# State-space units of a hybrid decoder step: outputs kept feature-major, their norm taken from column sums

## The reference, cut to what matters

```python
def step(s, inp):
    xb, dtb, dab, bb, cb = inp
    cum = jnp.cumsum(dab, axis=1)
    seg = cum[:, :, None] - cum[:, None, :]
    lmask = jnp.exp(jnp.where(causal, seg, -jnp.inf))
    cbw = jnp.einsum('bign,bjgn->bijg', cb, bb)
    wgt = cbw[..., None] * lmask * dtb[:, None]
    y = jnp.einsum('bijgr,bjgrp->bigrp', wgt, xb)
    y = y + jnp.einsum('bign,bgrpn->bigrp', cb, s) * jnp.exp(cum)[..., None]
    wlast = jnp.exp(cum[:, -1:] - cum) * dtb
    s = s * jnp.exp(cum[:, -1])[..., None, None] + jnp.einsum('bjgr,bjgrp,bjgn->bgrpn', wlast, xb, bb)
    return s, y
...
ys = ys + w['ssd_d'][l][:, None] * xs
gated = ys * jax.nn.silu(s_z)
y_c = _rmsnorm(gated, ssd_norm_g)      # over the 256 features of a group
```

## Time and profile before

| | before |
|---|---|
| median of 3 runs | 2722.2 us |
| profiled execution, its own time | 2716.7 us |
| its span, first to last instruction | 2714.6 us |
| mean granted TensorE clock | 0.996 of full |
| PE busy | 2672.4 us (98%) |
| weight loads busy | 2625.4 us |
| DVE busy | 1976.1 us (73%) |
| ACT busy | 894.2 us (33%) |
| POOL busy | 1254.0 us (46%) |

### The profile page before, as it was taken

One profiled execution on the slowest core, in us unless ns is written; L12 is line 12 of the kernel. 1 busy time (PEld: TensorE's weight loads), 2 busy tenths in 40 slices (PEclk: granted clock), 3 DMA queues, 4 the chain that ended last, 5 costly groups with the idle time before them and its releaser, 6 DMA issues.

```text
span 2714.6 us, 51113 instructions
## 1 busy us (share of the span) xinstructions
PE 2672.4 (98%) x18801; PEld 2625.4 (97%) x18801; DVE 1976.1 (73%) x2490; ACT 894.2 (33%) x1428; POOL 1254.0 (46%) x732
## 2 busy tenths in 40 slices
PE   9999999999999999999999999999999999999997
PEld 9999999989999999999999999999999999999997
DVE  7658887478866676667946598875787766677778
ACT  4443241134322232223424432312343322232333
POOL 2334233222665666666433333232226666666663
PEclk9999999999999999999999999999999999999999
DMA  4324333321211111111223344244111111111112
GB/s 165 129 77 158 137 114 127 118 65 32 64 54 47 47 47 47 54 54 47 71 87 104 113 141 143 84 141 134 42 47 48 47 47 60 49 47 47 47 62 92
DMA packets 74103, 219.60 MB, mean 81 GB/s; under 512 B 18480, under 2 KB 20144, under 8 KB 72896
## 3 DMA queue, kind: packets, MB, share of 16 engines
q1 hardware_dynamic: 69584, 202.27, 23.0%
q10 hardware_dynamic: 4368, 15.33, 1.9%
HBM read 176.35 MB, written 41.73 MB: 80 GB/s over the span
## 4 chain that ended last, share of the span: by engine, by line
PE 66%; issue 14%; POOL 8%; DVE 8%; DMA 2%; ACT 1%; PEld 1%; POOLq 0%; DVEq 0%; SPq 0%; ACTq 0%
PE ps L909 20%; PE ps L911 19%; PE ps L910 19%; POOL sb_w_lo L812 6%; DVE sb_pt L1950 2%; DMA sb_w_raw<-w 1%; DVE sb_x L1940 1%; PE ps L1043 1%; POOL sb_w_raw L855 1%; POOL sb_wsum L844 1%; PE ps L1158 1%; PE ps L1078 1%; PE ps L1079 1%; POOL sb_w_raw L851 1%; PE ps L1080 1%
## 5 line engine op out<-in xcount | busy, mean ns | idle before, releaser
L812 POOL TENSOR_TENSOR sb_w_lo<-sb_w_raw,sb_w_hi 128x512 fp32r<-128x512 f32 (+1 forms) x348 | 633.6, 1826 | 428.3 <-ACT sb_w_hi L1738 420.6
L909 PE MATMUL ps<-sb_p_hi,sb_w_hi 128*128 128x258 f32 (+1 forms) x2528 | 728.9, 288 | 7.2 <-POOL sb_w_lo L812 6.6
L911 PE MATMUL ps<-sb_p_hi,sb_w_lo 128*128 128x258 f32 (+1 forms) x2528 | 726.4, 287 | 0.0
L910 PE MATMUL ps<-sb_p_lo,sb_w_hi 128*128 128x258 f32 (+1 forms) x2528 | 725.8, 287 | 0.0
L809 POOL TENSOR_TENSOR sb_w_hi<-sb_w_raw,sb_ones 128x1024 fp32r<-128x1024 f32 (+1 forms) x92 | 180.4, 1961 | 846.7 <-PEq L906 733.8
L909 PE MATMUL ps<-sb_h_hi,sb_w_hi 128*128 128x344 f32 x1632 | 533.7, 327 | 4.1 <-DVE sb_h_lo L1902 1.6
L910 PE MATMUL ps<-sb_h_lo,sb_w_hi 128*128 128x344 f32 x1632 | 522.5, 320 | 0.0
L911 PE MATMUL ps<-sb_h_hi,sb_w_lo 128*128 128x344 f32 x1632 | 521.1, 319 | 0.0
L909 PEld LDWEIGHTS ps<-sb_p_hi,sb_w_hi 128*128 128x128 f32 x2528 | 478.0, 189 | 8.9 <-POOL sb_w_lo L812 7.6
L910 PEld LDWEIGHTS ps<-sb_p_lo,sb_w_hi 128*128 128x128 f32 x2528 | 479.4, 190 | 0.0
L911 PEld LDWEIGHTS ps<-sb_p_hi,sb_w_lo 128*128 128x128 f32 x2528 | 478.2, 189 | 0.0
(11 more groups left out here) (334 smaller groups left out, 3678.5 us busy)
## 6 DMA issues: line engine op xcount, KB each, us to landing
sb_w_raw<-w SPq DMA_DIRECT2D x178, 512.0 KB, 3.9
proj<-sb_ev SPq DMA_DIRECT2D x56, 516.0 KB, 3.0
sb_rawx<-w SPq DMA_DIRECT2D x44, 512.0 KB, 3.5
sb_pt<-proj SPq DMA_DIRECT2D x20, 516.0 KB, 5.2
sb_raw<-proj SPq DMA_DIRECT2D x16, 516.0 KB, 4.8
sb_raw<-proj ACTq DMA_DIRECT2D x16, 516.0 KB, 4.3
sb_ch<-cumT SPq DMA_DIRECT2D x32, 256.0 KB, 4.1
sb_raw<-ssd_state SPq DMA_DIRECT2D x4, 1024.0 KB, 6.2
```

Of the source, the lines that this page charges most:

```text
L812: return nc.gpsimd.tensor_tensor(o, a, h.bitcast(F32), ALU.subtract)
L909: mm(o, wh, ah, start=first, stop=False)
L910: mm(o, wh, al, start=False, stop=False)
L911: return mm(o, wl, ah, start=False, stop=last)
```

## The change

The outputs of a state-space unit stay feature-major. In `b_ssd` the values are stationary (128 x 64 for one head) and the segment weights are streamed (128 columns); of two heads one writes PSUM partitions 0 to 63 and the other 64 to 127. The state is stationary in two halves of 128 features, with C streamed. The two gate transposes are gone, and the wait for the gates moves from PE to DVE. ACT makes one more exponential for each chunk, `E(c)`, the decay laid out by features, in two activations of 64 partitions, ahead of the four Relu. DVE no longer makes `skip`, and adds D times the values with two fused operations. ACT's squares are written over the gates. The tail of u = 2 and 3 is new (`tail_s`): a column sum of squares by 9 small matmuls, root and reciprocal, 9 transposes that spread the result over the partitions, one scaling from PSUM, then the split. The retention units keep their tail.

```diff
         def b_ssd(u, c):
             s = cols(c)
             pe.wait_ge(*sg.after("awork", (u, c)))
-            if c == 0:
-                pe.wait_ge(*sg.after("gate_act", u))
-            else:
+            if c > 0:
                 pe.wait_ge(*sg.after("bwork", (u, c - 1)))
             for h in range(4):
-                mm(ps[:, 6, 64 * h:64 * h + 64], W(c)[:, 128 * h:128 * h + 128], xdt(c)[:, 64 * h:64 * h + 64],
+                j, q = h // 2, slice(64 * (h % 2), 64 * (h % 2) + 64)
+                mm(ps[q, 6, 128 * j:128 * j + 128], xdt(c)[:, 64 * h:64 * h + 64], W(c)[:, 128 * h:128 * h + 128],
                    start=True, stop=True)
-            mm(ps[:, 6, 256:512], pt[:, 1, s], St, start=True, stop=True)
             for j in range(2):
-                nc.tensor.transpose(ps[:, 7, 256 + 128 * j:384 + 128 * j], pt[:, Z0[u] + j, s], ident)
+                mm(ps[:, 6, 256 + 128 * j:384 + 128 * j], St[:, 128 * j:128 * j + 128], pt[:, 1, s], start=True, stop=True)
             mm(ps[:, 7, 0:256], btok(c), xwl(c), start=True, stop=True).then_inc(*sg.on("b_done", (u, c)))
...
+        def tail_s(u):
+
+            pe.wait_ge(*sg.after("sq_ready", u))
+            for c in range(NCH + 1):
+                n = min(CHUNK, T - c * CHUNK)
+                ins = mm(ps[0:n, 7, c:c + 1], pt[:, Z0[u], c * CHUNK:c * CHUNK + n], ones[:, 0:1], start=True, stop=True)
+            ins.then_inc(*sg.on("tok_sum", ("ssd", u)))
+            weights_done()
+            run(PLAN[u]["t"])
+            pe.wait_ge(*sg.after("tok_rstd", ("ssd", u)))
+            for c in range(NCH + 1):
+                n = min(CHUNK, T - c * CHUNK)
+                ins = nc.tensor.transpose(rstd_wide[:, c * CHUNK:c * CHUNK + n], rr[0:n, c:c + 1].to_broadcast([n, P]),
+                                          ident[0:n, 0:n])
+            ins.then_inc(*sg.on("tok_spread", ("ssd", u)))
+            weights_done()
...
         def seg_exp(u, c):
 
             act.wait_ge(*sg.after(f"seg_loaded{c % 3}", (u, c)))
+            if c >= 3:
+                act.wait_ge(*sg.after("bwork", (u, c - 3)))
+            for q in range(2):
+                rows = slice(64 * q, 64 * q + 64)
+                ins = af(halves(E(c))[rows], W(c).rearrange("p (j q n) -> p j q n", j=2, q=2)[rows, :, q, :], ACT.Exp)
+            ins.then_inc(*line.step())
+            act.wait_ge(*line.last())
             for h in range(4):
...
         def square_s(u, c):
-            act.wait_ge(*sg.after("bwork", (u, c)))
-            if c > 0:
-                act.wait_ge(*line.last())
-            af(junk.rearrange("p (j n) -> p j n", j=2), xt(u)[:, :, cols(c)], ACT.Square,
-               accum_out=ss[:, c:c + 1]).then_inc(*line.step())
+            if c < NCH:
+                act.wait_ge(*sg.after("bwork", (u, c)))
+                rows = cols(c)
+            else:
+                act.wait_ge(*sg.after("ys_ready", u))
+                rows = d
+            af(pt[:, Z0[u]:Z0[u] + 2, rows], xt(u)[:, :, rows], ACT.Square).then_inc(*sg.on("sq_done", (u, c)))
...
         def b_work_s(u, c):
             dve.wait_ge(*sg.after("b_done", (u, c)))
-            t = xwl(c)
-            v.tensor_tensor(heads(t, 4), heads(ps[:, 6, 256:512], 4),
-                            tk_of(1, u, c).unsqueeze(2).to_broadcast([P, 4, 64]), ALU.mult)
-            v.tensor_tensor(skip(c), skip(c), ps[:, 6, 0:256], ALU.add)
+            t, o = halves(xwl(c)), xt(u)[:, :, cols(c)]
+            v.tensor_tensor(t, halves(ps[:, 6, 256:512]), halves(E(c)), ALU.mult)
+            for j in range(2):
+                stt(o[:, j, :], o[:, j, :], A("ssd_d", 2 * u - 4 + j), ps[:, 6, 128 * j:128 * j + 128], ALU.mult, ALU.add)
...
+            if c == 0:
+                dve.wait_ge(*sg.after("gate_act", u))
             dve.wait_ge(*line.last())
-            v.tensor_tensor(xt(u)[:, :, cols(c)], heads(t, 2), heads(ps[:, 7, 256:512], 2),
-                            ALU.mult).then_inc(*sg.on("bwork", (u, c)))
+            v.tensor_tensor(o, o, pt[:, Z0[u]:Z0[u] + 2, cols(c)], ALU.mult).then_inc(*sg.on("bwork", (u, c)))
...
+        def tail_s(u):
+            sum_squares(u, d, NCH).then_inc(*sg.on("sq_ready", u))
+            dve.wait_ge(*sg.after("tok_sum", ("ssd", u)))
+            v.tensor_scalar(rr[:, 0:NCH], ps[:, 7, 0:NCH], 1.0 / 256, EPS, ALU.mult, ALU.add)
...
+            v.reciprocal(rr[:, 0:NCH + 1], rr[:, 0:NCH + 1]).then_inc(*sg.on("tok_rstd", ("ssd", u)))
+            run(PLAN[u]["t"])
+            dve.wait_ge(*sg.after("tok_spread", ("ssd", u)))
+            for j in range(2):
+                o = xt(u)[:, j, :]
+                stt(o, o, A("ssd_g", 2 * u - 4 + j), rstd_wide, ALU.mult, ALU.mult).then_inc(*sg.on("scaled", (u, j)))
+            if u == 2:
+                conv_s(3, 0)
+            elif u == 3:
+                rope(4, 0)
+            for j in range(2):
+                dve.wait_ge(*sg.after("y_hi", (u, j)))
+                ins = v.tensor_tensor(y_lo[:, j, :], xt(u)[:, j, :], y_hi[:, j, :].bitcast(F32), ALU.subtract)
+            ins.then_inc(*sg.on("y_split", u))
```

More of the change, by code:

```diff
@@ L327, in build, with E, halves @@
     St, junk = ch[:, 3072:3328], ch[:, 3328:3584]
-    def skip(c):
-        return ch[:, 2816:3072] if c % 2 == 0 else skip2[:]
+    def E(c):
+        return (ch[:, 2816:3072], ch[:, 3328:3584], skip2[:])[c % 3]
+    def halves(ap):
+        return ap.rearrange("p (j n) -> p j n", j=2)
+    rstd_wide = ps[:, 4:7, :].rearrange("p a n -> p (a n)")[:, 0:T]
     def kd(c):
@@ L582, in prep_early @@
                 if u > 3:
-                    sp.wait_ge(*sg.after("ys_turned", u - 1))
+                    sp.wait_ge(*(sg.after("tok_sum", ("ssd", 3)) if u == 4 else sg.after("ys_turned", u - 1)))
                     step()
@@ L597, in prep @@
                 if u < 4:
-                    sp.wait_ge(*(sg.after("y_split", 1) if u == 2 else sg.after("ys_turned", 2)))
+                    sp.wait_ge(*(sg.after("y_split", 1) if u == 2 else sg.after("tok_sum", ("ssd", 2))))
                     step()
@@ L1517, in square_r @@
             ins.then_inc(*sg.on("sq_done", (u, c)))
[L1519 to L1529, removed]
+        def tail_s(u):
+            square_s(u, NCH)
             act.wait_ge(*sg.after("rr_ms", u))
-            n = NCH + 1 if u < 4 else 2 * NCH + 2
-            af(rr[:, 0:n], rr[:, 0:n], ACT.Sqrt).then_inc(*sg.on("rr_root", u))
+            af(rr[:, 0:NCH + 1], rr[:, 0:NCH + 1], ACT.Sqrt).then_inc(*sg.on("rr_root", u))
             if u == 2:
@@ L1536, in tail @@
             y_free(u)
+            for j in range(2):
+                act.wait_ge(*sg.after("scaled", (u, j)))
+                af(y_hi[:, j, :], xt(u)[:, j, :], ACT.Identity).then_inc(*sg.on("y_hi", (u, j)))
+        def tail(u):
+            act.wait_ge(*sg.after("sy_ready", u))
+            act.wait_ge(*sg.after("sq_done", (u, NCH - 1)))
+            for h in range(2):
+                ins = af(junk[0:8, 128 * h:128 * h + 128], ps[0:8, 6, 128 * h:128 * h + 128], ACT.Square,
+                         accum_out=ss[0:8, 16 + h:17 + h])
+            ins.then_inc(*sg.on("ss_done", u))
+            act.wait_ge(*sg.after("rr_ms", u))
+            n = 2 * NCH + 2
+            af(rr[:, 0:n], rr[:, 0:n], ACT.Sqrt).then_inc(*sg.on("rr_root", u))
+            y_free(u)
             yh, _ = Y(u)
-            g = A("ssd_g", 2 * u - 4, 2) if u < 4 else A("ret_g", 2 * (u - 4), 2)
+            g = A("ret_g", 2 * (u - 4), 2)
             r = RING["tail", u]
@@ L2085, in b_work_r, with sum_squares @@
                             ALU.mult).then_inc(*sg.on("o_gated", (u, c)))
+        def sum_squares(u, rows, c):
+            dve.wait_ge(*sg.after("sq_done", (u, c)))
+            return v.tensor_tensor(pt[:, Z0[u], rows], pt[:, Z0[u], rows], pt[:, Z0[u] + 1, rows], ALU.add)
         def decode_s(u):
@@ L2428, in _ @@
                     decode_r(u)
-                tail(u)
+                if u < 4:
+                    tail_s(u)
+                else:
+                    tail(u)
             def gp(m):
```

83 lines of the change are left out of this document (38 added, 45 removed).

## The result

The changed kernel takes **2731.3 us** (median of 8 runs, 2721.9 to 2735.4), the kernel before 2722.0 (8 runs, 2717.7 to 2727.1). The ratio is 1.0027, with a 95% interval of 1.0016 to 1.0038: slower by 7.3 us, at least 4.4 and at most 10.3. The forecast was 2726.6 with a range of 2715 to 2736: the time is inside. The likeliest outcome by its chances, a change of at most 0.2%, is just missed: it is 0.27%, with an interval that reaches to both sides of that line.

The account below looks back on a forecast made before the run. PE, busy for 98% of the span, was taken as the bound, with DVE next in the chunks. Chunks -10.2, first chunk +1.7, tails +6.5 and clock +6.4 made +4.4: 2722.2 + 4.4 = 2726.6 us, range 2715 to 2736.

Parts of the forecast that it names:

- Chunks, PE: PE in the 32 state-space chunks: head products cheaper, gate transposes gone, 0.32 us saved a chunk, -10.2 us.
- DVE follows; I charge nothing: State-space chunks: DVE, already full, loses its slack but follows PE's 0.32 gain; charged nothing, up to 2 us for the range.
- DVE becomes the bound of the chunks: Rival: DVE bounds the chunks, or the next units start late; +2 to +6 on the forecast, 2729 to 2733; chance 0.08.
- DVE: forecast -0.26 a chunk: DVE in the chunks: `skip` goes, its add becomes two fused operations of some 0.20 us each; net -0.26 us a chunk.
- First chunk: First chunk of u = 2: two activations and a wait lengthen PE's wait by 0.87 us in each layer, +1.7.
- Tails: Four tails of u = 2 and 3: wait +0.94, sums +1.9, turn back replaced by spread -1.2, +6.5 in all.
- Clock: After the four tails: idleness and one-column passes in a row lower the clock at nearly every one, 1.6 us each, +6.4.
- the second rival: Behind the tails: the clock falls twice at each; +10.8, 2733 us; chance 0.15.
- The first rival: In the tails: the clock stays up; -2.0, 2720.2 us; chance 0.15.
- at most +1 each: Behind the tails: DVE's two scalings delay the next unit's work by up to 2 us; charged nothing, at most +1 each.
- DVE's 1032-column work in the tail: Tails: DVE's sum of 1024 columns costs nothing, at most 0.3; its two scalings, some 1.15 us each, also charged nothing.
- 0.07: Rival in the chunks' head products: the two heads do not run side by side; sum +19.1, 2741 us; chance 0.07.

Follow-up runs that it names:

- experiment 2: Changed kernel with all four heads' products written by the same half of the array's columns, even heads' results left out: 2742.3 us, one run.
- experiment 3: Changed kernel with two head products of 128 stationary columns in place of four of 64, array left whole: 2728.0 us, one run.
- experiment 4: Changed kernel without the two extra exponentials, state product and DVE's share of it in each state-space unit's first chunk: 2723.0 us, ratio 0.9996 to the kernel before.
- experiment 1: Changed kernel with the four head products in the order 0, 2, 1, 3: 2728.8 us, ratio 1.0023 to the kernel before.
- experiment 5: Changed kernel with 12 unread filler matmuls of 344 columns ahead of PE's wait for the squares in each state-space tail: 2725.2 us, ratio 1.0009 to the kernel before.
- experiment 6: Changed kernel with one product of nine columns in place of the nine column sums, the wait kept: 2716.9 us, ratio 0.9979 to the kernel before.
- experiment 7: Changed kernel with one of the tail's two in pieces run before the column sums, on PE and DVE: 2713.9 us, ratio 0.9975 to the kernel before.
- Experiment 8: Kernel of experiment 7 with ones stationary and squares streamed, no spreading transposes, root and reciprocal over 1032 columns: 2744.1 us, ratio 1.0077 to the kernel before.

## Why the prediction was right, and where it wasn't

- **Chunks, PE: forecast -10.2, traces -7.4.** The price itself was right: 1.67 us for 1.65, halves side by side (experiment 2), 0.33 for the way in and out (experiment 3; 0.35 in the sum). u = 3 gave -2.45 of -2.56. What failed is the step "DVE follows; I charge nothing". u = 2 gave -1.26, since PE waited 1.1 us for DVE before the fourth chunk; half of that is DVE, which POOL's split held up for 0.5 us longer than before, and half is PE's own gain (experiment 4). And behind the fourth chunk of both units PE waits some 0.4 us more than before. That makes 3.8 us for 2.8 that the chunks are short; the 1.0 between came back elsewhere in the chunks and is not assigned. It is the rival "DVE becomes the bound of the chunks" (chance 0.08) beside the forecast's case, at the low end of its +2 to +6.
- **DVE: forecast -0.26 a chunk.** The two fused products start 0.26 apart, not 0.20, so the net is -0.15. Against PE's 0.32 DVE loses 0.17 us of slack a chunk, where the forecast had 0.06.
- **First chunk: forecast +1.7, trace +1.9.** Right, and experiment 4 took it away.
- **Tails: forecast +6.5.** The wait 0.87 x 4 for 0.94 x 4. Behind the first sum the four tails cost 12.95 more; less six stretches of 1.6 that leaves 3.35, forecast 2.8. In all 6.8: right, but in part by luck. 1.5 of the 3.35 are PE waiting 0.7 us for an eviction of u = 3 (line 1970) behind each tail of u = 2, which was charged at nothing, "at most +1 each"; sums and spread leave 1.9 of their 2.8.
- **Clock: forecast +6.4, four falls; trace +9.6, six.** Every tail brought a fall, as said; those of u = 2 brought two in succession in the profiled execution (one each in that of experiment 1), which was the second rival (chance 0.15). So the truth lay between forecast and rival. The reason given, wait and sums in a row, fits experiments 5 to 7; the wait alone was never enough, and the sums alone were in three places of eight. The first rival, that the clock stays up, is what experiment 7 had to arrange. The Trainium skill (TensorE: Matmul & The Clock Gate, "Why this matters for your kernels") warns of idle gaps alone; by that rule a gap of 1.9 us does nothing, and experiment 6 agrees. But one-column passes without a gap brought falls in experiment 5, and there the measurement decides.
- **The sum.** The terms of the two traces make -7.4 + 1.9 + 6.8 + 9.6 = +10.9 for +4.4: 2.8 of the miss are the chunks of u = 2, 3.2 the second falls. The ratio says +7.3, only 2.9 more than forecast, and by it the first three terms leave 6.0 for the clock. That would fit executions of before that have more falls than the profiled one (35 of them in one comparison lie between 2715.4 and 2730.5), but it is worked out by difference and not shown.
- **DVE's 1032-column work in the tail: charged at nothing, nearly right.** Its scalings are hidden but for the waits of 0.7 above. Experiment 8 shows how thin that cover is.
- **The chances.** Those named as slower by over 0.2% (0.15, 0.07, 0.08 and a quarter of 0.43) add up to 0.41, not 0.34, which leaves 0.43 for no change: a slip in the addition, and slower is what came.

Still open: why the sums alone brought the clock down in experiment 5 and not in 7, where PE was as busy ahead of them; four tails each are few, and the times of 7 (2711.8 to 2714.0 in seven runs, 2719.8 to 2721.4 in three) let me suppose that some of its runs had falls too. That wasn't looked at.

## What to carry to other kernels

A gain on PE is only as large as the slack of the engine that follows it: look for the operation that does not fit between two of the neighbour's, not at its mean busy share. A reduction that needs a result of a slow engine belongs behind work that is already there; moving it by one piece was worth 14 to 17 us, more than the 10.2 that the chunks were to give. And where the starting state is zero, leave the term out.

## What the runs showed of the hardware

- A DVE product whose operands all lie in SBUF was held up while POOL worked there: 0.69 us became 2.75 (267.67 above, POOL at work from 267.47 to 269.87). Where DVE began first, in before at 267.62, its 0.68 us stayed, and POOL's operation took 2.86 for 2.40. At the tail of u = 3 a product of 16 columns took 2.28 us beside a split, the timelines of DVE and of POOL in after:

```profile
439.68 2.28 DVE L2162 TENSOR_TENSOR sb_xt<-sb_xt,sb_pt 128x16 f32<-128x16 f32 x1
```

```profile
439.56 2.37 POOL L817 TENSOR_TENSOR sb_w_lo<-sb_w_raw,sb_w_hi 128x1024 fp32r<-128x1024 f32 x1
```

The Trainium skill (GPSIMD Engine Reference, "1. Specifications") names contention for the SBUF interfaces where DVE has two SBUF inputs. The trace agrees, and shows its size: nearly the whole of POOL's operation. So part of the 1.72 us wait for the sums is this product; but it took 2.29 us in before too, so it is no part of the 0.87 that the change added there.
- Passes in the two column halves started within 7 to 13 ns of each other in both orders of issue, and going into the halves and back cost 0.33 us a chunk (experiment 3).
- A reciprocal of 1032 columns cost 6.4 ns a column on DVE, five times a fused product.
